# A two-block transformer forward pass on one core: the order in which the first modulation tiles, the query latents and the context's sum of squares run

## The chip, the cores and the metric

One core of a Trainium2 chip runs the whole kernel. The metric is the device time of one execution in microseconds (us). Engines: TensorE (PE in the profile, its weight loads PEld), VectorE (DVE), ScalarE (ACT), GpSimd (POOL), and the queue SP, which only issues transfers here.

## What is computed

The reference runs two transformer blocks over 256 tokens of width 1024, all in float32. The first block, cut to what matters here:

```
sh1, sc1, g1, sh2, sc2, g2 = split(silu(c) @ w_mod + b_mod)          # w_mod is 1024 x 6144
csh1, csc1, ...            = split(silu(c_ctx) @ w_mod + b_mod)
hx = rmsnorm(x,   g_attn) * (1 + sc1)  + sh1                         # 256 x 1024
hc = rmsnorm(ctx, g_attn) * (1 + csc1) + csh1                        # 256 x 1024
q_lat, na_q                      = split(hx @ w_in[:, :896])         # 384 + 512, queries: x alone
kv_lat, k_rope, na_k, na_v       = (hx and hc) @ w_in[:, 896:]       # 256 + 32 + 512 + 512
q = rmsnorm(q_lat) @ w_uq;  k, v = rmsnorm(kv_lat) @ w_ukv
attention (latent and neighbourhood), output projection, 16-expert MoE
```

The second block (spatial gating, forgetting attention, a convolutional feed-forward) follows. The change touches only the start: everything up to `kv_lat`.

## The kernel before

Activations lie feature-major: `xT` and `ctxT` are 8 tiles (`KD = 8`, index k) of 128 features by 256 tokens. Weights stream from HBM through a ring of six slots of 2 MiB (`ring`, `slot_of`); the queue SP issues the loads in a written order, and before a slot is used again it waits until its last reader is done (`through`). Slot 2 and the upper half of slots 0 and 1 share memory with early activations.

The products with `w_in` keep float32 accuracy in three fast passes: ScalarE rounds a chunk of 1024 weights per partition to a high part (`chunk_to_hi`, L619), VectorE makes the rest (`chunk_to_lo`, low part L1690), and TensorE runs high x high, low x high, high x low (`tile_product`, L1037). The activation is split in the same way: VectorE scales (`normed`, L1727), ScalarE adds the shift and rounds (`shifted`, L631), VectorE makes the low part (`shifted_lo`, L1734). A query tile has 256 columns, a tile of keys or values has 512 (x and context side by side).

At the start, in the order of the engines' programs:

- SP issues xT, the four modulation tiles `w_mod[0..3]` (shift of features 0 to 511, shift of 512 to 1023, then scale of the same two), ctxT, the part `ql` of `w_in` (384 columns, 1536 KB, into the slot of `w_mod[0]`), `kvl`, the constants, `naq`, and so on.
- TensorE multiplies a modulation tile with silu(c) and silu(c_ctx) (`mod_stream`, L978: 8 products in four column strips), each tile into a bank of its own. ScalarE copies a bank out (L612), TensorE sums the strips and puts features on partitions with a two-column matrix (`mod_pick`, L987). After the first tile it sums the squares of x with a matrix of ones (L997), after the last pick the squares of the context (L997 again), whose squares VectorE made (L1710).
- VectorE then forms `mod` (L1713) and `A1` (L1715) for all 8 tiles at once, scales x, makes the low parts of three weight chunks, makes the low parts of x, and does the same for the context.
- The list `PROD` sets the order of the products: 3 query latent tiles (`ql`), 2 key-value latent tiles (`kvl`), the rope keys (`kr`), 4 neighbourhood query tiles (`naq`), 4 of keys (`nak`), then values, and the second level. The result of product n goes to bank n % 4 and is copied out by ScalarE or VectorE ("A" or "D" in the list) before product n + 4 may write it. Chunk c + 4 is split once the product that used chunk c is done.

Of the kernel before, what the change touches and what calls it, by code (L numbers as in the profile page):

```python
# [5 lines left out]
P = 128  # L6
T = 256
# [28 lines left out]
L_QL, L_KVL, L_NAQ, L_NAK, L_NAV, L_UQ, L_UKV = range(4, 11)  # L36
# [37 lines left out]
def columns(widths):  # L74
    at, out = 0, {}
    for name, w in widths:
# [9 lines left out]
CON, NCON = columns([("upper", 128), ("ones", 128), ("pick", 2), ("pick8", 8), ("pick20", 20), ("ident", 128), ("tri", 128),  # L86
# [6 lines left out]
PROD = ([("ql", i, "AD"[i % 2]) for i in range(3)] + [("kvl", 0, "D"), ("kvl", 1, "A"), ("kr", 0, "D")]  # L93
        + [("naq", i, "AD"[i % 2]) for i in range(4)]
# [5 lines left out]
N_BEFORE_LAT = 10  # L100
W_IN = {"ql": (0, QL), "kvl": (QL, 288), "naq": (QL + 288, 512), "nak": (QL + 800, 512), "nav": (QL + 1312, 512)}
# [83 lines left out]
def block_pair_kernel(nc, xT_d, ctxT_d, vec_d, row_d, con_d, w_mod, w_in, w_uq, w_ukv, bias_d, w_out,  # L185
                      wr_d, w_gate, w_up, w_down, w_in2, wf_d, sgw_d, w_out2, w_up2, w_down2, gfin_d, out_d):
    with ExitStack() as ctx:
# [123 lines left out]
        pick = con[:, CON["pick"]:CON["pick"] + 2]  # L311
# [52 lines left out]
        squares, squared = [sem("squares0")], sem("squared")  # L364
# [46 lines left out]
        def through(n):  # L411
# [4 lines left out]
            if n < 4:  # L416
                return mod_streamed, n + 1
# [14 lines left out]
            return wide_lo, 4 * (n - L_UP + 1)  # L432

# [23 lines left out]

        NAV_DONE = [p[:2] for p in PROD].index(("nav", 3)) + 1
        UQ_FIRST = [p[:2] for p in PROD].index(("ur", 0))


        @block.sync
        def _(sp):
            def issue(n, src, cols=SLOT):
# [3 lines left out]
                sp.dma_start(ring[:, slot_of(n), 0:cols], src).then_inc(  # L468
# [13 lines left out]
            issue(L_NAQ, *w_in_part("naq"))  # L482
# [58 lines left out]
        def _(pool):  # L541

# [46 lines left out]
        def _(act):  # L589
# [17 lines left out]
            nc.scalar.activation(hT[:, :, 0:T], xT[:, :, :], ACT.Square).then_inc(squares[0], 1)  # L607
            act.wait_ge(var, NORM_STEP[0] + 1)
            nc.scalar.activation(rstd[:, 0:T], rstd[:, 0:T], ACT.Sqrt).then_inc(std, 1)
            for half in range(4):  # L610
                act.wait_ge(mod_streamed, half + 1)
                nc.scalar.activation(modp[:, half * 512:(half + 1) * 512], bank[half][:, :], ACT.Copy  # L612
                                     ).then_inc(mod_copied, 1)
# [8 lines left out]
            for c in range(3):  # L622
                chunk_to_hi(0, CHUNK1, c)
# [340 lines left out]
        def _(pe):  # L964
            def slot(n, k):

                return ring[:, slot_of(n), 0:SLOT // k * k].rearrange("p (k n) -> p k n", k=k)
# [1364 lines left out]
```

## Time and profile before

| what | value |
|---|---|
| median of 3 runs | 834.27 us (831.6 to 839.86) |
| the profiled execution's own time | 834.69 us |
| its span in the profile | 832.9 us |
| mean granted TensorE clock over the span | 0.972 of full speed |
| PE busy | 783.2 us (94%) |
| DVE / ACT / POOL busy | 394.8 / 309.4 / 21.7 us |
| moved by DMA | 198.89 MB, mean 239 GB/s |

Some 1.8 us of the execution's time lie outside the span. Rows of a timeline give start, duration, engine, line, operation, output <- inputs and count; in brackets, how long the engine had been idle and what released it. A matmul in float32 appears as two instructions. "DMA share" is the busy share of the 16 DMA engines; "PEclk" is the clock that TensorE was granted, 1.00 being 2.4 GHz and 0.50 being 1.2 GHz.

### The profile page before, as it was taken

How to read it: one execution, taken by the hardware profiler on the slowest of the kernel's cores; microseconds unless marked ns; L12 is line 12 of the kernel's file. 1: busy time of each engine (PE TensorE's matmuls, PEld its weight loads, DVE VectorE, ACT ScalarE, POOL GpSimd, SP SyncE). 2: the span in 40 equal slices, each digit the busy share in tenths (PEclk: the TensorE clock that was granted, in tenths of full speed). 3: DMA queues.
4: the chain of work that ended last, by engine and by line, in shares of the span. 5: the costliest groups of instructions: out<-in, count | busy, mean ns of one | idle time of the engine just before them, and what ended most of it. 6: DMA issues, size and time to landing. Idle time of an engine off the chain costs nothing.

```text
span 832.9 us, 11883 instructions
## 1 busy us (share of the span) xinstructions
PE 783.2 (94%) x4693; PEld 562.7 (68%) x4694; DVE 394.8 (47%) x709; ACT 309.4 (37%) x564; POOL 21.7 (3%) x22
## 2 busy tenths in 40 slices
PE   4899999999996999999999999998799999999997
PEld 1588884444784535553554448886698999999885
DVE  0685404578544101111110126766646788888543
ACT  2453103556533101100110125655344666666443
POOL 0000010030000000000000000010000000000000
PEclk9999999999996999999999998999898999999999
DMA  9934113986266799999999994204300455475401
GB/s 377 417 124 196 55 46 119 357 318 242 102 252 260 308 384 430 430 428 429 429 429 428 427 428 188 102 1 160 144 26 13 191 203 201 172 297 237 152 0 52
DMA packets 15637, 198.89 MB, mean 239 GB/s; under 512 B 1744, under 2 KB 2128, under 8 KB 3184
## 3 DMA queue, kind: packets, MB, share of 16 engines
q1 hardware_dynamic: 14688, 194.80, 57.9%
q0 software_dynamic: 624, 3.28, 1.0%
q8 instruction: 26, 0.43, 0.2%
q10 hardware_dynamic: 288, 0.30, 0.1%
q14 instruction: 11, 0.09, 0.0%
HBM read 197.31 MB, written 1.05 MB: 238 GB/s over the span
## 4 chain that ended last, share of the span: by engine, by line
PE 81%; DMA 6%; DVE 6%; ACT 5%; issue 1%; DVEq 0%; SPq 0%; ACTq 0%
PE banks L1383 12%; PE banks L1037 8%; PE banks L1641 7%; PE banks L1409 6%; PE banks L1616 5%; PE banks L1624 5%; PE banks L1620 5%; PE banks L1354 4%; PE banks L1365 3%; DMA ring<-in_w_up 3%; PE banks L1185 3%; DVE w_lo L1690 2%; PE banks L978 2%; DMA ring<-in_w_in 2%; ACT w_hi L619 2%; PE banks L1205 2%
## 5 line engine op out<-in xcount | busy, mean ns | idle before, releaser
L1690 DVE TENSOR_TENSOR w_lo<-ring,w_hi 128x1024 fp32r<-128x1024 f32 x119 | 144.8, 1223 | 92.0 <-ACT w_hi L619 44.9
L1383 PE MATMUL banks<-ring,att 128*64 128x512 f32 x512 | 111.7, 593 | 3.3 <-DVE att L2001 2.0
L1383 PEld LDWEIGHTS banks<-ring,att 128*64 128x64 f32 x512 | 36.7, 137 | 76.4 <-issue 73.1
L619 ACT ACTIVATE w_hi<-ring 128x1024 fp32r<-128x1024 f32 x53 | 54.9, 1052 | 42.4 <-PE banks L1037 28.2
L1409 PE MATMUL banks<-ring,att 128*64 128x512 f32 x256 | 56.7, 595 | 0.6 <-DVE att L2016 0.6
L2014 DVE TENSOR_TENSOR att<-att,banks 128x512 f32<-128x512 f32 x8 | 5.5, 688 | 103.6 <-PE banks L1383 103.6
L1616 PE MATMUL banks<-h_hi,w_hi 128*128 128x256 f32 x352 | 51.7, 287 | 0.3 <-ACT h_hi L913 0.3
L890 ACT ACTIVATE w_hi<-ring 128x1024 fp32r<-128x1024 f32 x44 | 46.2, 1052 | 14.1 <-PE banks L1624 14.1
L1624 PE MATMUL banks<-h_lo,w_hi 128*128 128x256 f32 x352 | 50.2, 286 | 0.0
L1620 PE MATMUL banks<-h_hi,w_lo 128*128 128x256 f32 x352 | 49.8, 284 | 0.0
L1616 PEld LDWEIGHTS banks<-h_hi,w_hi 128*128 128x128 f32 x352 | 46.3, 194 | 2.0 <-ACT h_hi L913 1.2
L1624 PEld LDWEIGHTS banks<-h_lo,w_hi 128*128 128x128 f32 x352 | 46.2, 195 | 0.0
L1620 PEld LDWEIGHTS banks<-h_hi,w_lo 128*128 128x128 f32 x352 | 45.7, 193 | 0.0
L1409 PEld LDWEIGHTS banks<-ring,att 128*64 128x64 f32 x256 | 17.7, 137 | 33.6 <-issue 32.8
L978 PE MATMUL banks<-ring,cs 128*32 128x512 f32 x192 | 26.0, 665 | 13.8 <-DMA ring<-in_w_mod 13.8
L1365 PE MATMUL banks<-arena,osb 128*128 (+1 forms) x256 | 32.1, 287 | 4.1 <-DVE arena L1986 4.1
L791 ACT ACTIVATE arena<-banks 128x256 f32 (+1 forms) x8 | 3.1, 384 | 86.8 <-PE banks L1395 86.8
L1354 PEld LDWEIGHTS banks<-arena 128*128 128x128 f32 x144 | 26.6, 190 | 11.6 <-issue 8.3
L1354 PE MATMUL banks<-arena 128*128 (+1 forms) x144 | 33.5, 385 | 1.0 <-DVE arena L2021 1.0
L1365 PEld LDWEIGHTS banks<-arena,osb 128*128 128x128 f32 x256 | 31.3, 203 | 4.3 <-DVE arena L1986 4.3
L789 ACT ACTIVATE att<-banks 128x512 f32<-128x512 f32 x8 | 4.8, 597 | 76.9 <-PE banks L1383 76.9
L895 ACT ACTIVATE w_hi<-ring 128x1024 fp32r<-128x1024 f32 x22 | 23.2, 1059 | 26.9 <-PE banks L1641 25.9
(339 smaller groups left out, 1377.9 us busy)
## 6 DMA issues: line engine op xcount, KB each, us to landing
ring<-in_w_up SPq DMA_DIRECT2D x27, 2048.0 KB, 13.4
ring<-in_w_down SPq DMA_DIRECT2D x21, 2048.0 KB, 12.3
ring<-in_w_gate SPq DMA_DIRECT2D x16, 2048.0 KB, 13.3
ring<-in_w_mod SPq DMA_DIRECT2D x12, 2048.0 KB, 9.7
ring<-in_w_in SPq DMA_DIRECT2D x8, 2048.0 KB, 13.6
ring<-in_w_out SPq DMA_DIRECT2D x4, 2048.0 KB, 7.9
arena<-in_bias POOLq DMA_DIRECT2D x2, 1024.0 KB, 9.9
ring<-in_w_in SPq DMA_DIRECT2D x1, 1536.0 KB, 18.2
```

What stands on the lines that cost most here:

```text
L619: nc.scalar.activation(chunk_part(w_hi, chunk, c), chunk_src(chunk, c), ACT.Copy).then_inc(chunk_hi[stage], 1)
L890: nc.scalar.activation(granule(w_hi, j, half), up_half_of(j, half), ACT.Copy).then_inc(wide_hi, 1)
L1037: last = nc.tensor.matmul(dst, chunk_part(part, chunk, c)[:, k, :], x[:, k, :], start=(part is w_hi and x is x_hi and k == 0), stop=(x is ...
L1354: last = nc.tensor.matmul(yacc(m), ysb[:, m * P:(m + 1) * P], place[:, i, :], start=False, stop=False, skip_group_check=True)
L1365: last = nc.tensor.matmul(bank[k // 4][:, (k % 4) * P:(k % 4 + 1) * P], h2tok[:, q, k * P:(k + 1) * P], arena[:, bass.ds(at + q * 1024, P) ...
L1383: last = nc.tensor.matmul(bank[2 + j][CAP * e:CAP * (e + 1), :], xs[:, k, CAP * e:CAP * (e + 1)], slot(n + e, KD)[:, k, :], start=(k == 0) ...
L1409: last = nc.tensor.matmul(bank[2 + half][CAP * e:CAP * (e + 1), :], hidT[:, f, CAP * e:CAP * (e + 1)], slot(L_MOE + 4 + e, 4)[:, f, half * ...
L1616: nc.tensor.matmul(dst, granule(w_hi, j, g)[:, k, :], h2_hi[:, k, :], start=(k == 0), stop=False)
L1620: nc.tensor.matmul(dst, granule(w_lo, j, g)[:, k, :], h2_hi[:, k, :], start=False, stop=False)
L1624: last = nc.tensor.matmul(dst, granule(w_hi, j, g)[:, k, :], h2_lo[:, k, :], start=False, stop=(k == KD - 1))
L1641: return nc.tensor.matmul(ytok(q, half)[:, :], x[:, kt, q * P:(q + 1) * P], part[:, kt // 2 % 2, kt % 2, half * 512:(half + 1) * 512], sta ...
L1690: return V.tensor_tensor(dst, src, high.bitcast(F32), ALU.subtract)
```

## The change

- The modulation tiles are loaded and multiplied in the order 0, 2, 1, 3 (`MOD_ORDER`): shift and scale of the first 512 features, then shift and scale of the last 512. The two tiles of a half go to the same bank, the second two rows lower (`row` = 2), so that one copy and one pick with a four-column matrix (`pick4`) serve both. The third tile loaded goes to the upper half of `arena` (`home`).
- `ql` is loaded ahead of the modulation tiles, and `naq` ahead of `kvl`. In `PROD`, `naq` stands ahead of `kvl` and `kr`. The slots up to the experts move on by one accordingly.
- The squares of x are summed ahead of all modulation tiles. VectorE makes the low parts of the three `ql` chunks ahead of the modulation, then forms `mod` and `A1`, scales and splits x by halves (k = 0 to 3, then 4 to 7). TensorE runs the first half of the first query latent tile between tile 2 and tile 3 of the modulation, the first halves of the other two between tile 3 and tile 4, and the second halves behind the last pick.
- The context's squares are made on ScalarE (between the second copy of the modulation and the shifts of k = 4 to 7), summed over k on GpSimd in three steps (4, 2 and 1 tiles of 256 columns), and only the last tile goes through TensorE, behind the third query latent product (n = 3). The context is scaled and split by VectorE and ScalarE while the `naq` products run.
- The sums of the latents' squares come ahead of product 12, not 10.

The diff, cut to its core:

```diff
-L_QL, L_KVL, L_NAQ, L_NAK, L_NAV, L_UQ, L_UKV = range(4, 11)
+L_QL, L_MOD, L_NAQ, L_KVL, L_NAK, L_NAV, L_UQ, L_UKV = 0, 1, 5, 6, 7, 8, 9, 10
+MOD_ORDER = (0, 2, 1, 3)
-        return (3, 4, 5, 2,  3, 4, 5, 3, 4, 5, 3,  4, 5, 3, 4, 5, 3, 4, 5,  3, 4)[n]
+        return (3,  4, 5, 2, 4,  5, 3, 4, 5, 3, 4,  5, 3, 4, 5, 3, 4, 5, 3,  4, 5)[n]
-PROD = ([("ql", i, "AD"[i % 2]) for i in range(3)] + [("kvl", 0, "D"), ("kvl", 1, "A"), ("kr", 0, "D")]
-        + [("naq", i, "AD"[i % 2]) for i in range(4)]
+PROD = ([("ql", i, "AD"[i % 2]) for i in range(3)] + [("naq", i, "AD"[i % 2]) for i in range(4)]
+        + [("kvl", 0, "D"), ("kvl", 1, "A"), ("kr", 0, "D")]
-N_BEFORE_LAT = 10
+N_BEFORE_LAT = 12
+        def home(n):
+            return arena[:, 4096:8192] if n == L_MOD + 2 else ring[:, slot_of(n), :]
             sp.dma_start(xT[:, :, :], xT_d).then_inc(in_x, 16)
+            issue(L_QL, *w_in_part("ql"))
             for n in range(4):
-                issue(n, w_mod[n])
+                issue(L_MOD + n, w_mod[MOD_ORDER[n]])
             sp.dma_start(ctxT, ctxT_d).then_inc(in_ctx, 16)
-            issue(L_QL, *w_in_part("ql"))
+            issue(L_NAQ, *w_in_part("naq"))
             issue(L_KVL, *w_in_part("kvl"))
...
+            for n in (4, 2, 1):
+                pool.wait_ge(ctx_sq, {4: 1, 2: 2, 1: 3}[n])
+                nc.gpsimd.tensor_tensor(hT[:, 0:n, T:2 * T], hT[:, 0:n, T:2 * T], hT[:, n:2 * n, T:2 * T], ALU.add
+                                        ).then_inc(ctx_sq, 1)
...
+            def mod_copy(half):
+                act.wait_ge(mod_streamed, 2 * half + 2)
+                nc.scalar.activation(modp[:, half * 512:(half + 1) * 512], bank[4 + half], ACT.Copy).then_inc(mod_copied, 1)
+            for c in range(3):
+                chunk_to_hi(0, CHUNK1, c)
+            mod_copy(0)
+            shift(0, range(4))
+            mod_copy(1)
+            act.wait_ge(in_ctx, 16)
+            nc.scalar.activation(hT[:, :, T:2 * T], ctxT, ACT.Square).then_inc(ctx_sq, 1)
+            shift(0, range(4, KD))
+            chunk_to_hi(0, CHUNK1, 3)
...
             for n, (kind, i, e) in enumerate(PROD):
-                if n == 5:
+                if n == 2:
+                    act.wait_ge(var, NORM_STEP[0] + 2)
+                    nc.scalar.activation(rstd[:, T:2 * T], rstd[:, T:2 * T], ACT.Sqrt).then_inc(std, 1)
+                if n == 3:
+                    shift(1, range(KD))
+                if n == KVL_FIRST + 2:
...
+            pe.wait_ge(silu_c, 1)
+            pe.wait_ge(in_con, 16)
+            pe.wait_ge(x_sq, 1)
+            for k in range(KD):
+                last = nc.tensor.matmul(bank[7][:, 0:T], ones, hT[:, k, 0:T], start=(k == 0), stop=(k == KD - 1))
+            last.then_inc(sumsq, 1)
+            mod_stream(L_MOD, 4, 0, True, False)
+            mod_stream(L_MOD + 1, 4, 2, False, True)
+            mod_pick(0)
+            latent_q(0, range(4))
+            mod_stream(L_MOD + 2, 5, 0, True, False)
+            latent_q(1, range(4))
+            latent_q(2, range(4))
+            mod_stream(L_MOD + 3, 5, 2, False, True)
+            mod_pick(1)
             for n, (kind, i, _e) in enumerate(PROD):
+                if n == 3:
+                    pe.wait_ge(ctx_sq, 4)
+                    nc.tensor.matmul(bank[7][:, T:2 * T], ones, hT[:, 0, T:2 * T], start=True, stop=True).then_inc(sumsq, 1)
...
-            dve.wait_ge(in_ctx, 16)
-            V.tensor_tensor(hT[:, :, T:2 * T], ctxT, ctxT, ALU.mult).then_inc(squares[0], 1)
...
+            for c in range(3):
+                chunk_to_lo(0, CHUNK1, c)
...
+            for half in range(2):
+                modulation(half)
+                scaled_by_norm(0, range(4 * half, 4 * half + 4))
+                shifted_low(0, range(4 * half, 4 * half + 4))
+            chunk_to_lo(0, CHUNK1, 3)
...
             for n, (kind, i, e) in enumerate(PROD):
+                if n == 2:
+                    dve.wait_ge(sumsq, SUMMED[0] + 2)
+                    V.tensor_scalar(rstd[:, T:2 * T], bank[7][:, T:2 * T], 1.0 / D, EPS, ALU.mult, ALU.add
+                                    ).then_inc(var, 1)
+                if n == 3:
+                    dve.wait_ge(std, NORM_STEP[0] + 2)
+                    link(V.reciprocal(rstd[:, T:2 * T], rstd[:, T:2 * T]))
+                    scaled_by_norm(1, range(KD))
+                if n == 4:
+                    shifted_low(1, range(KD))
```

## Rows read from the trace of the kernel before

**Rows 1.** Windows of the first 60 us and of one MoE stretch: length, busy (instructions), PEclk, DMA share, GB/s

```profile
5.00:10.00 5.00, 0.00 (x0) 0.00 (x0) 0.24 (x2) 3.24 (x3) 0.00 (x0) 1.00 1.02 429
20.00:25.00 5.00, 4.77 (x44) 2.39 (x36) 1.75 (x1) 1.69 (x4) 0.00 (x0) 1.00 1.02 436
35.00:40.00 5.00, 4.52 (x15) 2.55 (x14) 5.00 (x8) 5.00 (x11) 0.00 (x0) 0.94 1.06 440
50.00:60.00 10.00, 10.00 (x68) 7.59 (x70) 6.64 (x9) 4.06 (x6) 0.00 (x0) 1.00 0.01 2
296.00:325.00 29.00, 29.00 (x154) 14.25 (x152) 3.88 (x9) 3.08 (x7) 0.00 (x0) 1.00 0.96 399
```

**Rows 2.** Timeline, 38 to 54 us: query latent tiles, context, the first key-value tile

```profile
38.32 3.25 DVE L1734 SCALAR_TENSOR_TENSOR hT_lo<-arena,mod,hT_hi 128x256 fp32r<-128x256 f32 x8
...
42.09 1.12 PE L1037 MATMUL banks<-hT_hi,w_hi 128*128 128x256 f32 x8
42.95 1.75 DVE L1724 RECIPROCAL rstd<-rstd 128x256 f32<-128x256 f32 x1
...
44.97 1.12 PE L1037 MATMUL banks<-hT_hi,w_hi 128*128 128x256 f32 x8
...
47.84 2.00 PE L1037 MATMUL banks<-hT_hi,w_hi 128*128 128x512 f32 x8
...
53.31 1.98 PE L1037 MATMUL banks<-hT_hi,w_hi 128*128 128x512 f32 x8
```

**Rows 3.** Timeline, 0 to 34 us: what the transfers release

```profile
1.21 0.45 ACTq L599 DMA_DIRECT2D con<-in_con  x1
...
6.86 1.89 ACT L607 ACTIVATE arena<-xT 128x2048 f32<-128x2048 f32 x1
11.97 3.47 PE L978 MATMUL banks<-ring,cs 128*32 128x512 f32 x16 [11.97 <-DMA ring<-in_w_mod]
...
26.56 1.92 PE L978 MATMUL banks<-ring,cs 128*32 128x512 f32 x16 [1.79 <-DMA ring<-in_w_mod]
...
29.10 2.29 DVE L1710 TENSOR_TENSOR arena<-osb 128x2048 f32<-128x2048 f32 x1 [7.30 <-DMA osb<-in_ctxT]
...
33.75 2.95 ACT L619 ACTIVATE w_hi<-ring 128x1024 fp32r<-128x1024 f32 x3 [4.60 <-DMA ring<-in_w_in]
```

**Rows 4.** Timeline, 15 to 38 us: sums of squares, modulation, scaling and splitting of x

```profile
15.37 3.72 PE L997 MATMUL banks<-arena,con 128*128 128x256 f32 x16
...
28.41 1.95 PE L987 MATMUL banks<-con,mixT 128*128 128x2 f32 x16
28.55 0.60 ACT L612 ACTIVATE mixT<-banks 128x512 f32<-128x512 f32 x1 [4.10 <-PE banks L978]
...
31.31 0.18 DVE L1713 TENSOR_TENSOR mod<-banks,vec 128x32 f32<-128x32 f32 x1
31.45 5.41 PE L997 MATMUL banks<-arena,con 128*128 128x256 f32 x16 [1.08 <-DVE arena L1710]
...
31.74 3.26 DVE L1727 SCALAR_TENSOR_TENSOR arena<-xT,A,rstd 128x256 f32<-128x256 f32 x8
...
36.61 3.29 ACT L631 ACTIVATE hT_hi<-arena,mod 128x256 fp32r<-128x256 f32 x8
```

**Rows 5.** DMA issues of the first 1.5 us: output <- input, queue, count, KB, us to landing

```profile
con<-in_con ACTq DMA_DIRECT2D x1, 143.0 KB, 10.8
```

**Rows 6.** GpSimd additions of 2048 and 1024 elements per partition, by source line (ns)

```profile
L565 POOL TENSOR_TENSOR arena<-arena,con x2: 3801/3930/4058, 167.3 to 184.4; 128x2048 f32<-128x2048 f32 x2
```
```profile
L578 POOL TENSOR_TENSOR arena<-arena,con x1: 1997/1997/1997, 549.0 to 549.0; 128x1024 f32<-128x1024 f32 x1
```

**Rows 7.** Timeline: VectorE without and beside a GpSimd addition

```profile
166.81 0.88 DVE L1829 TENSOR_SCALAR att<-att,rinv 128x512 f32<-128x512 f32 x2
...
184.40 3.80 POOL L565 TENSOR_TENSOR arena<-arena,con 128x2048 f32<-128x2048 f32 x1 [8.55 <-DMA arena<-in_bias]
...
184.57 4.31 DVE L1829 TENSOR_SCALAR att<-att,rinv 128x512 f32<-128x512 f32 x2
```

**Rows 8.** Timeline: VectorE beside a GpSimd addition, one input in PSUM

```profile
549.46 1.29 DVE L1690 TENSOR_TENSOR hid_hi<-banks,hid_lo 128x512 fp32r<-128x512 f32 x2 [1.65 <-ACT hid_lo L871]
```

**Rows 9.** Windows around a fall of the granted clock

```profile
25.70:29.10 3.40, 2.54 (x22) 1.10 (x23) 0.00 (x0) 0.55 (x1) 0.00 (x0) 1.00 1.03 430
29.10:31.40 2.30, 1.26 (x12) 1.17 (x11) 2.30 (x2) 0.05 (x1) 0.00 (x0) 1.00 1.00 419
31.40:35.60 4.20, 4.15 (x12) 3.36 (x13) 4.13 (x11) 1.85 (x2) 0.00 (x0) 0.60 1.00 408
```

**Rows 10.** Timeline: VectorE's first and last instructions of the latents' norm

```profile
75.66 0.42 DVE L1791 TENSOR_SCALAR mixT<-banks 128x256 f32<-128x256 f32 x1 [0.37 <-PE banks L1022]
...
84.06 1.40 DVE L1801 SCALAR_TENSOR_TENSOR lat<-lat,vec,mixT 128x512 f32<-128x512 f32 x2
```

More of the change, by code:

```diff
@@ L606, in _ @@
             act.wait_ge(in_x, 16)
-            nc.scalar.activation(hT[:, :, 0:T], xT[:, :, :], ACT.Square).then_inc(squares[0], 1)
+            nc.scalar.activation(hT[:, :, 0:T], xT[:, :, :], ACT.Square).then_inc(x_sq, 1)
             act.wait_ge(var, NORM_STEP[0] + 1)
             nc.scalar.activation(rstd[:, 0:T], rstd[:, 0:T], ACT.Sqrt).then_inc(std, 1)
[L610 to L613, printed above, removed]
             def chunk_to_hi(stage, chunk, c):
@@ L985, in mod_pick @@
                 for t in range(4):
-                    c = 8 * half + 2 * t
-                    last = nc.tensor.matmul(bank[6][:, c:c + 2], modp[:, (4 * half + t) * P:(4 * half + t + 1) * P], pick,
+                    at = 16 * half + 4 * t
+                    last = nc.tensor.matmul(bank[6][:, at:at + 4], modp[:, (4 * half + t) * P:(4 * half + t + 1) * P], pick4,
                                             start=True, stop=True)
                 last.then_inc(mod_picked, 1)
-            pe.wait_ge(silu_c, 1)
-            def square_sum(part):
-                pe.wait_ge(squares[0], part + 1)
-                at = slice(part * T, (part + 1) * T)
-                for k in range(KD):
-                    last = nc.tensor.matmul(bank[7][:, at], ones, hT[:, k, at], start=(k == 0), stop=(k == KD - 1))
-                last.then_inc(sumsq, 1)
-            for half in range(4):
-                mod_stream(half, half)
-                if half == 0:
-                    pe.wait_ge(in_con, 16)
-                    square_sum(0)
-                else:
-                    mod_pick(half - 1)
-            mod_pick(3)
-            square_sum(1)
             def bank_free(prod, n, sa, sd):
@@ L1026, in _, with tile_product @@
             loads = {"ur": L_UQ, "kn": L_UKV, "vm": L_UKV}
-            def tile_product(stage, chunk, c, dst, x_hi, x_lo, hi_done, lo_done, passes=range(3)):
+            def tile_product(stage, chunk, c, dst, x_hi, x_lo, hi_done, lo_done, passes=range(3),
+                             ks=range(KD)):
                 pe.wait_ge(chunk_hi[stage], c + 1)
@@ L1033, in tile_product @@
                         pe.wait_ge(chunk_lo[stage], c + 1)
-                    for k in range(KD):
+                    for k in ks:
                         if done is not None:
@@ L1717, in _ @@
-            for s in range(2):
-                if s == 1:
-                    dve.wait_ge(sumsq, SUMMED[0] + 2)
-                    V.tensor_scalar(rstd[:, T:2 * T], bank[7][:, T:2 * T], 1.0 / D, EPS, ALU.mult, ALU.add
-                                    ).then_inc(var, 1)
-                    chunk_to_lo(0, CHUNK1, 3)
-                    dve.wait_ge(std, NORM_STEP[0] + 2)
-                    link(V.reciprocal(rstd[:, T:2 * T], rstd[:, T:2 * T]))
-                for k in range(KD):
-                    src = (xT, ctxT)[s][:, k, :]
-                    V.scalar_tensor_tensor(hT[:, k, s * T:(s + 1) * T], src, A1[:, k, s:s + 1],
+            for c in range(3):
+                chunk_to_lo(0, CHUNK1, c)
@@ new lines, in modulation, with block @@
+            def modulation(half):
+                def block(t):
+                    return t.rearrange("p (i u) c -> p i u c", i=2)[:, :, 4 * half:4 * half + 4, :]
+                dve.wait_ge(mod_picked, half + 1)
+                link(V.tensor_tensor(block(mod[:, 0:16, :]),
+                                     bank[6][:, 16 * half:16 * half + 16].rearrange("p (t i c) -> p i t c", t=4, i=2),
+                                     block(bc(v_("b_mod", 0, 16), 2, [P, 16, 2])), ALU.add))
+                ks = slice(4 * half, 4 * half + 4)
+                link(V.scalar_tensor_tensor(A1[:, ks, :], mod[:, 8 + 4 * half:12 + 4 * half, :], 1.0,
+                                            bc(v_("g_attn", 4 * half, 4), 2, [P, 4, 2]), ALU.add, ALU.mult))
```

78 lines of the change are left out of this document (35 added, 43 removed).

## The prediction

> **What bounds the kernel now.** I read the page first (PE busy 94% of the span), then windows of the start, then the timeline of that stretch, and last the windows of the MoE. For its first 40 us the core takes all that the DMA engines give, 429 to 440 GB/s at a share of 1.0, and TensorE works in pieces between arrivals; from about 40 us TensorE is busy all the time, and DMA idles [rows 1]. The reader should see the handover: until then a transfer sets the pace, afterwards every product that starts earlier ends earlier. In the MoE stretch TensorE is again full; in the code its loads wait for `used`, which TensorE raises when it is through with a slot, so a shift at the start moves them too and is carried to the end [rows 1]. So the place to measure is the moment at which the query latent tiles are done and nothing but full TensorE work follows: 47.84 us, when the first key-value tile starts [rows 2].
>
> What leads there is a chain of transfers. The first modulation tile releases TensorE at 11.97, the fourth at 26.56, the context at 29.10, `ql` only at 33.75 [rows 3]. One 2048 KB tile therefore takes (26.56 - 11.97) / 3 = 4.86 us. Then come three weight chunks on ScalarE (2.95 us) and eight shifts behind them, the first at 36.61 [rows 3, 4]; x's scaling was done at 35.0. The sum of the context's squares (31.45 to 36.86, [rows 4]) is just not late.
>
> **The change, part by part.**
>
> Transfers. `ql` in front costs the modulation 1536/2048 x 4.86 = 3.65 us: first tile at 11.97 + 3.65 = 15.6, then 20.5, 25.3 and 30.2. The matrix of ones is needed first now; it was issued at 1.21 and took 10.8 us [rows 5], so it is there at about 12. The squares of x are ready by 8.75 [rows 3], their sum takes 3.72 us at full clock and, estimated by the first stream's slowness (3.47 against 1.92 us, [rows 3]), some 1.6 more: done at 17.3, still 3 us ahead of the second tile. The fourth tile's slot is free when the first is streamed (17.3 + 1.9 = 19.2), while two tiles are queued until 25.3, so SP's wait leaves no gap. The context lands at about 32.7, `naq` at 37.6, `kvl` at 40.3, each ahead of its use below. The load into `arena` touches nothing in use. Cost of all this: nothing, hidden by the queue; if the fourth tile came over 3 us late, that would be added.
>
> First half. Tile 2 is streamed at 20.5 + 1.9 = 22.4. Before, from the end of the last stream (28.48) to the last pick's end (30.36) went 1.9 us; from the start of `mod` (31.31) to that of scaling (31.74) 0.43 [rows 3, 4]. Four scalings take 4 x 0.41 = 1.6, four low parts as much (8 in 3.26 and 3.25, [rows 2, 4]), and TensorE ends 0.3 behind: 1.9 + 0.1 + 0.4 + 1.6 + 1.6 + 0.3 = 6.0 us, so 28.4. ScalarE's three chunks (17.9 to 20.9) and VectorE's reciprocal and three low parts (to about 23.5) hide under the tile's arrival.
>
> Middle. Stream 1.9, two half tiles, stream 1.9. A query tile takes 44.97 - 42.09 = 2.88 us [rows 2], so two halves take 2.9. Together 6.7, so the fourth stream ends at t0 = 35.1, 5 us behind the tile's arrival: TensorE, not DMA, sets this.
>
> Second half. The same 6.0 us and two halves, 2.9: 44.0. Against 47.84 that is 3.8 us gained. The single context product (one of eight: 3.72/8 = 0.46 us, [rows 4]) is added: 3.4 left. Half the picks and the sum of 5.41 us vanish, but they stood under the transfer, so they count nothing more.
>
> Context squares. On ScalarE the square takes 1.89 us (as x's, [rows 3]) from the second copy's end: t0 + 0.7 to t0 + 2.6. The shift of k = 4, queued behind it, is not ready before t0 + 2.9, so this wait is covered by 0.3 us. GpSimd then adds 1024, 512 and 256 elements. 1024 take 2.00 us, 2048 take 3.80 to 4.06 [rows 6]; by the same slope the others take 1.05 and 0.55, together 3.6, ending at t0 + 6.3, while TensorE asks at t0 + 8.9. For TensorE they are hidden by 2.6 us. For VectorE they are not. Beside GpSimd's addition of 184.40 to 188.20, two tensor_scalars that take 0.88 alone took 4.31: VectorE stood until the addition was over [rows 7]. The adds start at t0 + 2.65, in the middle of VectorE's four scalings (from t0 + 2.4), on which the shifts, the low parts and TensorE wait. No row shows a scalar_tensor_tensor beside an addition. The lower bound is nothing, by the product pair that read PSUM and took 1.29 us beside an addition, 0.64 for 512 elements where 256 take 0.41 elsewhere [rows 2, 8]; the upper is all three adds, 3.6. I take 3.6: scalings read two SBUF operands and no PSUM, which is nearer to [rows 7] than to [rows 8], and each add is asked for while a scaling runs and follows it.
>
> The Trainium skill (SBUF — State Buffer, "Who interferes with whom") says that a VectorE instruction with two SBUF inputs contends with a GpSimd instruction that reads SBUF, and that the second to issue blocks until the first is done. The trace agrees for the tensor_scalar (4.31 us); that the two-input form does the same no row shows. By the rule the sum is the one here; without it, that of the first rival.
>
> Clock. In 29.10 to 31.40 TensorE did 1.26 us, all of it two-column picks, and over 31.40 to 35.60 the granted clock was 0.60 in the mean, so at 1.2 GHz for most of it [rows 9]; the sum of squares took 5.41 for 3.72, 1.7 us more [rows 4]. The stretch with a whole stream in it (25.70 to 29.10) brought no fall [rows 9]. The changed kernel has two such holes: 22.4 to 28.4, and t0 to t0 + 9.5 with the adds. In each TensorE does a few picks and products that wait for ScalarE. Bounds are 0 and 1.7 for each. The first falls partly under work that is paced by ScalarE anyway: 0.7. The second is longer and is followed by full work: 1.7. Together 2.4.
>
> Context chain. Behind the third query tile VectorE and ScalarE must do the variance, square root, chunk, reciprocal (1.75), eight scalings (3.26), a shift, chunk and copy. That is some 11.3 us, under four `naq` tiles of 4 x 2.88 = 11.5 [rows 2, 4]. Their cover is 0.2 us thick; bounds 0 and 1.5, I take 0.2, since bank 0 too comes free at about the moment when the second key-value tile asks for it. Behind it the latents' sums come two products later. VectorE's norm of the latents (75.66 to 85.46, 9.8 us, [rows 10]) stood under two tiles of keys and stands under the other two now, each 53.31 - 47.84 = 5.47 us [rows 2]: 10.9 us and then the rope products, with the first two value chunks split already. Cost nothing; its cover is 1 us and more.
>
> Sum: -3.8 + 0.4 + 3.6 + 2.4 + 0.2 = +2.8 us. Against the profiled execution (834.69) that is 837.5; it lay 0.4 above the median of the runs, so against the median 837.0.
>
> **The rivals.**
>
> 1. VectorE is not held. For it: [rows 8]. Against it: [rows 7]. Without 3.6, and with a shorter second hole (clock 0.7 + 0.6): -3.8 + 0.4 + 1.3 + 0.2 = -1.9, so 832.4. If the clock also stays up, 831.1.
> 2. GpSimd waits for VectorE instead: VectorE's instructions follow each other at once, and the adds start when its low parts are done, t0 + 5.8. They end at t0 + 9.4, TensorE's context product waits 0.5 us, the clock costs 1.9: -3.8 + 0.4 + 0.5 + 1.9 + 0.3 = -0.7, so 833.6. For it: no row shows an addition asked for amid VectorE's back-to-back work and winning.
> 3. Slower: the context chain becomes the bound. Its place is the first key-value tile (n = 7), which needs the context's shifts, chunk 7 and bank 3. It decides as soon as the chain is longer than the 11.5 us of `naq`; every us beyond is added. With the chain stretched by waits of both engines for each other's chunks (one more chunk on each, 1.0 + 1.2, and 1 us for the second tile's bank) it gives 3.2 more: 840.2. Against it: ScalarE is idle for half of such stretches [rows 1].
> 4. The change doesn't do what it says: the latents' first halves start so late that the fourth tile is streamed no earlier than `ql` was used before. The fourth tile's 5 us of slack speak against it; it would give 838 to 842.
>
> **How the numbers follow.** Forecast 0.50, rival 1 0.25, rival 2 0.12, rival 3 0.10, rival 4 0.03. The range runs from rival 1 with the clock kept (831.1) less half a us for the spread of runs, to rival 3 plus as much: 830.5 to 841.0. A measurement of this kernel can tell about 1% (8.3 us) from no change; no case passes that but for its tail, so faster 0.03, within 0.93, slower 0.04.
>
> **What would show it.** In the changed profile: the first modulation stream near 16 to 17, the fourth ending near 35; a scaling that starts near 37.8 and whose group of four takes over 5 us instead of 1.6, beside three GpSimd additions; granted clock under 1.00 in 26 to 30 and again in 38 to 44; the third query latent product ending near 50, where without holding it would be near 45; the first key-value tile starting 12 us behind it, with no PE idle ahead of it. The distance from the end of `ql` to the attention should be unchanged but for 0.46. The prediction is wrong if VectorE runs through, if the clock stays at 1.00, or if a stage behind 143 us moves by itself.

## The result, and the profile after

| | before | changed |
|---|---|---|
| median of 15 runs each, us | 834.52 (831.6 to 839.86) | 842.3 (835.44 to 844.13) |
| profiled execution, us | 834.69 | 841.15 |
| its span, us | 832.9 | 839.4 |
| mean granted clock | 0.972 | 0.964 |

The ratio is 1.0074, 95% interval 1.0051 to 1.0097: slower by 6.2 us (4.3 to 8.1), where +2.8 was forecast. It is within 1%, and the sign was right; the size was less than half of what came. The prediction's range, up to 841.0, holds the ratio applied to its own starting median (1.0074 x 834.27 = 840.4) and just misses the later median of 842.3.

The page of the changed kernel: span, busy time of TensorE and of GpSimd, and the granted clock in 40 slices of 21 us. TensorE did the same work; GpSimd has 6.5 us more than the 21.7 of before, though the three new additions are only 4.5 of that.

```profile
span 839.4 us, 11817 instructions
...
PE 784.0 (93%) x4664; PEld 563.0 (67%) x4664; DVE 398.8 (48%) x710; ACT 310.1 (37%) x563; POOL 28.2 (3%) x25
...
PEclk9889999999996999999999998999888999999999
```

The timeline of the start (start, duration, engine, line). The modulation stream is L996 now, the sum of squares L1083 and, for the context alone, L1098; picks L1005, scaling L1753, low parts L1759, weight products L1038, ScalarE's square L644, GpSimd's additions L550.

```profile
10.59 5.28 PE L1083 MATMUL banks<-arena,con 128*128 128x256 f32 x16 [10.59 <-DMA con<-in_con]
15.80 1.92 PE L996 MATMUL banks<-ring,cs 128*32 128x512 f32 x16
20.15 3.21 PE L996 MATMUL banks<-ring,cs 128*32 128x512 f32 x16 [2.42 <-DMA ring<-in_w_mod]
24.06 1.05 PE L1005 MATMUL banks<-con,mixT 128*128 128x4 f32 x8 [0.70 <-ACT mixT L630]
25.57 1.67 DVE L1753 SCALAR_TENSOR_TENSOR arena<-xT,A,rstd 128x256 f32<-128x256 f32 x4
30.06 2.31 PE L996 MATMUL banks<-arena,cs 128*32 128x512 f32 x16
35.37 1.92 PE L996 MATMUL banks<-ring,cs 128*32 128x512 f32 x16
37.85 1.90 ACT L644 ACTIVATE arena<-osb 128x2048 f32<-128x2048 f32 x1
39.51 5.24 DVE L1753 SCALAR_TENSOR_TENSOR arena<-xT,A,rstd 128x256 f32<-128x256 f32 x4
39.84 4.63 POOL L550 TENSOR_TENSOR arena<-arena 128x1024 f32<-128x1024 f32 x3 [39.37 <-ACT arena L644]
44.68 1.66 DVE L1759 SCALAR_TENSOR_TENSOR hT_lo<-arena,mod,hT_hi 128x256 fp32r<-128x256 f32 x4
50.54 0.60 PE L1098 MATMUL banks<-arena,con 128*128 128x256 f32 x2
62.48 2.00 PE L1038 MATMUL banks<-hT_hi,w_hi 128*128 128x512 f32 x8
147.26 1.95 PE L1211 MATMUL banks<-arena,big 128*128 128x512 f32 x4 [0.83 <-issue]
```

Against [rows 2 to 4]: the four scalings of the first half take 1.67 us, the same four of the second half 5.24, over nearly the same stretch as GpSimd's additions. The query latents end at about 50.4 where they ended at 47.84, and attention (L1211) starts at 147.26 where L1185, the same line in the kernel before, started at 144.09: +3.2.

```profile
144.09 2.38 PE L1185 MATMUL banks<-arena,big 128*128 128x512 f32 x5 [0.83 <-issue]
```

The rest of the 6.2 us comes later.

The windows around the two stretches in which TensorE has little to do, for comparison with [rows 9]: us, then busy time of PE, PEld, DVE, ACT and POOL (instructions), granted clock, DMA share, GB/s.

```profile
17.80:20.15 2.35, 0.00 (x0) 0.00 (x0) 2.31 (x3) 1.83 (x2) 0.00 (x0) 1.00 1.05 446
20.15:23.40 3.25, 3.21 (x16) 0.54 (x16) 1.96 (x2) 0.00 (x0) 0.00 (x0) 0.58 0.98 418
...
26.70:30.00 3.30, 3.25 (x12) 2.65 (x12) 2.12 (x6) 1.09 (x3) 0.00 (x0) 0.62 0.96 407
40.60:45.30 4.70, 1.52 (x3) 0.76 (x3) 4.70 (x5) 1.53 (x4) 3.71 (x3) 0.56 1.04 370
45.30:47.40 2.10, 2.05 (x9) 2.06 (x10) 2.10 (x4) 0.94 (x1) 0.00 (x0) 0.50 0.93 398
```

The clock falls twice in the first 30 us: under the second stream, behind 2.35 us in which TensorE did nothing (granted clock 1.00 there, 0.58 in the stream), and again about 26.7. The groups of GpSimd's additions, kept apart by shape (busy us, mean ns of one):

```profile
L575 POOL TENSOR_TENSOR arena<-arena,con 128x2048 f32<-128x2048 f32 x2 | 9.1, 4530 | 19.1 <-DMA arena<-in_bias 19.1
L588 POOL TENSOR_TENSOR arena<-arena,con 128x1024 f32<-128x1024 f32 x1 | 2.4, 2414 | 304.0 <-ACT arena L845 304.0
...
L550 POOL TENSOR_TENSOR arena<-arena 128x1024 f32<-128x1024 f32 x1 | 2.4, 2360 | 39.4 <-ACT arena L644 39.4
L550 POOL TENSOR_TENSOR arena<-arena 128x512 f32<-128x512 f32 x1 | 1.3, 1331 | 0.1
L550 POOL TENSOR_TENSOR arena<-arena 128x256 f32<-128x256 f32 x1 | 0.8, 787 | 0.1
```

L575 and L588 are L565 and L578 of [rows 6], untouched by the change: they took 3930 and 1997 ns and take 4530 and 2414.

### The profile page after: what moved, and what is told of

Read it like the earlier page. It is cut to its first block, busy times and chain, and to the rows that moved or that the text cites. A ratio compares the mean times of both kernels' runs of the same rounds, so it can differ in the third digit from the quotient of the medians.

```text
span 839.4 us, 11817 instructions
## 1 busy us (share of the span) xinstructions
PE 784.0 (93%) x4664; PEld 563.0 (67%) x4664; DVE 398.8 (48%) x710; ACT 310.1 (37%) x563; POOL 28.2 (3%) x25
## 4 chain that ended last, share of the span: by engine, by line
PE 77%; DMA 10%; DVE 6%; ACT 5%; issue 1%; SPq 0%; DVEq 0%; ACTq 0%
PE banks L1409 11%; PE banks L1038 8%; DMA ring<-in_w_up 8%; PE banks L1667 7%; PE banks L1642 5%; PE banks L1646 5%; PE banks L1650 5%; PE banks L1435 4%; PE banks L996 3%; PE banks L1380 3%; PE banks L1211 3%; PE banks L1391 2%; DVE w_lo L1716 2%; DMA ring<-in_w_mod 2%; ACT w_hi L625 2%; PE banks L1220 2%
## 5 line engine op out<-in xcount | busy, mean ns | idle before, releaser
L1409 PE MATMUL banks<-ring,att 128*64 128x512 f32 x512 | 113.6, 600 | 3.1 <-DVE att L2042 2.0
L1435 PE MATMUL banks<-ring,att 128*64 128x512 f32 x256 | 56.7, 595 | 0.6 <-DVE att L2057 0.6
L1038 PE MATMUL banks<-hT_hi,w_hi 128*128 128x256 f32 (+1 forms) x104 | 23.8, 360 | 6.4 <-ACT hT_hi L635 6.4
```

The lines of the kernel that those rows point to most:

```text
L1038: last = nc.tensor.matmul(dst, chunk_part(part, chunk, c)[:, k, :], x[:, k, :], start=(part is w_hi and x is x_hi and k == 0), stop=(x is ...
L1409: last = nc.tensor.matmul(bank[2 + j][CAP * e:CAP * (e + 1), :], xs[:, k, CAP * e:CAP * (e + 1)], slot(n + e, KD)[:, k, :], start=(k == 0) ...
L1435: last = nc.tensor.matmul(bank[2 + half][CAP * e:CAP * (e + 1), :], hidT[:, f, CAP * e:CAP * (e + 1)], slot(L_MOE + 4 + e, 4)[:, f, half * ...
```

## The experiments

Differences in us are (ratio - 1) x 835; each kernel is compared with runs of the kernel before on its own chip.

### Do the additions hold VectorE?

**No additions.** The changed kernel with GpSimd's three additions left out; TensorE's single context product then takes the first 128 features' squares alone.

```
-            for n in (4, 2, 1): ... gpsimd.tensor_tensor(...)
-                    pe.wait_ge(ctx_sq, 4)
+                    pe.wait_ge(ctx_sq, 1)
```

> The three GpSimd additions of the context's squares are left out (the sum takes the squares of the first 128 features only, so the context's norm is another one); all else is as in the changed kernel. Theory (the additions hold VectorE's four scalings): the group of four scalings falls from 5.24 us to 1.67, the third query latent product ends about 3.6 us earlier or a little more by the clock (near 46.5 instead of 50.4), and the kernel takes about 4 to 5 us less than the changed one, 0 to +0.3% of the kernel before. Rival (the scalings are slow by their own place in the order, or the loss is made by the clock alone): the group stays over 4 us and the time within 1 us of the changed kernel, +0.7%.

Measured: 836.34 us, ratio 1.0012 [0.9982, 1.0041]. Timeline of the second half:

```profile
38.61 1.67 DVE L1749 SCALAR_TENSOR_TENSOR arena<-xT,A,rstd 128x256 f32<-128x256 f32 x4
...
46.16 0.60 PE L1094 MATMUL banks<-arena,con 128*128 128x256 f32 x2
```

The group takes 1.67 us again, 3.57 less than 5.24. From the fourth stream's end to the end of the query latents it is 46.04 - 36.38 = 9.66 us, where the changed kernel took 50.42 - 37.29 = 13.13: 3.47 less. So the holding is the whole of what this stretch loses to the additions: the longer hole that it makes costs at most 0.1 us of clock beyond.

**The square earlier.** In ScalarE's program the context's square goes ahead of the second copy of the modulation, so that the additions fall into the stretch before the scalings. Nothing is left out.

```
             mod_copy(0)
             shift(0, range(4))
-            mod_copy(1)
             act.wait_ge(in_ctx, 16)
             nc.scalar.activation(hT[:, :, T:2 * T], ctxT, ACT.Square).then_inc(ctx_sq, 1)
+            mod_copy(1)
             shift(0, range(4, KD))
```

> ScalarE squares the context ahead of the second copy of the modulation, when the context has landed (32.4), not behind it; the additions then start near 34.4 and end near 38.1. Theory: only the last 0 to 0.8 us of them meet the scalings (from 39.5 in the changed kernel, when the copy isn't delayed), the group takes 1.7 to 2.4 us, the third query latent product ends near 46.5 to 47, and the time is 3.5 to 5 us under the changed kernel's, -0.1 to +0.4% of the kernel before. Rival (what holds VectorE is any GpSimd work near it, or the additions cost elsewhere when moved, on the copy or on the weight chunks): the gain is under 1.5 us, at least +0.6% of the kernel before.

Measured: 835.4 us, ratio 1.0001 [0.9978, 1.0024]. Timeline:

```profile
32.48 1.91 ACT L643 ACTIVATE arena<-osb 128x2048 f32<-128x2048 f32 x1 [5.89 <-DMA osb<-in_ctxT]
...
34.48 4.50 POOL L550 TENSOR_TENSOR arena<-arena 128x1024 f32<-128x1024 f32 x3 [34.01 <-ACT arena L643]
...
38.27 2.17 DVE L1753 SCALAR_TENSOR_TENSOR arena<-xT,A,rstd 128x256 f32<-128x256 f32 x4
```

The same additions, the same work: only the 0.7 us at which the last addition overlaps the first scaling are held (2.17 for 1.67). The query latents end at 45.96, 1.9 us ahead of the kernel before.

**More additions.** Two more of 1024 elements ahead of the three, written to a free tile; the result is not changed. Shortened:

```
+            pool.wait_ge(ctx_sq, 1)
+            for n in range(2):
+                nc.gpsimd.tensor_tensor(att[...], hT[:, 0:4, T:2 * T], hT[:, 4:8, T:2 * T], ALU.add) ...
             for n in (4, 2, 1):
```

> Two more GpSimd additions of 1024 elements per partition (2.0 us each) into unused memory, ahead of the three. Theory: VectorE is held once more for each, so the scalings and the low parts of the second half take about 4 us more together, and the third query latent product ends 4 us later, near 54.4, the kernel at 4 to 5 us more than the changed one, +1.2 to +1.4% of the kernel before. Rival (GpSimd only got in once, before VectorE's queue was full): VectorE's groups stay as they are, and at most the context's product waits, for 1 us or less.

Measured: 844.2 us, ratio 1.0115 [1.0078, 1.0151]. Timeline:

```profile
38.53 7.93 DVE L1758 SCALAR_TENSOR_TENSOR arena<-xT,A,rstd 128x256 f32<-128x256 f32 x4
38.86 4.84 POOL L550 TENSOR_TENSOR att<-arena 128x1024 f32<-128x1024 f32 x2 [38.40 <-ACT arena L649]
...
43.78 4.69 POOL L555 TENSOR_TENSOR arena<-arena 128x1024 f32<-128x1024 f32 x3
```

VectorE gets one instruction in per addition: four scalings and the start of the low parts are stretched over five additions, 7.93 us for 1.67, and the low parts 3.15 for 1.66. The first key-value tile comes at 65.2, 2.7 later than in the changed kernel, in which the stage had started about 1 us later.

**TensorE sums the context.** The additions are left out and TensorE does all 8 products of the sum behind the third query latent.

```
-                    nc.tensor.matmul(bank[7][:, T:2 * T], ones, hT[:, 0, T:2 * T], start=True, stop=True)
+                    for k in range(KD):
+                        nc.tensor.matmul(bank[7][:, T:2 * T], ones, hT[:, k, T:2 * T], start=(k == 0), stop=(k == KD - 1))
```

> No GpSimd additions; TensorE sums all eight tiles of the context's squares behind the third query latent product, 3.7 us instead of 0.46. Theory: the 3.6 us of holding go, 3.3 us of TensorE come, the first key-value tile starts at about the same time or up to 1 us earlier for the shorter hole (61.5 to 62.4), and the time is within 1.5 us of the changed kernel's, +0.5 to +0.8% of the kernel before. Rival (holding isn't the loss): 3.3 us more than the changed kernel, +1.1%.

Measured: 840.85 us, ratio 1.0064 [1.0035, 1.0092]. Scalings take 1.67 us; the first `naq` product starts at 48.95, 1.8 before the changed kernel's. The eight products take 3.4 us (from the first weight load at 45.56 to the next product's at 48.92) where the single one took 0.3 (50.42 to 50.76), on an engine that is full from there on. The first key-value tile came at 60.65, ahead of the 61.5 to 62.4 that was expected. So moving the sum to GpSimd is worth having, if its additions lie where VectorE isn't wanted.

### What do the holes cost in clock?

**TensorE kept busy.** The early square and a shift of the constants (below), and 12 products of the matrix of ones with x into a bank that is free: four behind the first stream, one ahead of and three behind each of the two picks.

> As the kernel with both edits, with twelve further products of ones and x into an unused bank: four between the first two modulation tiles, one ahead of each pick, three behind each pick, 0.46 us each, in stretches where TensorE had waited. Theory (the clock falls because TensorE does little in these holes): the granted clock stays 1.00 from 16 us on, the third modulation stream takes 1.92 instead of 2.28 us and more, the first halves less, and the first key-value tile starts 1 to 2 us earlier than at 58.0; the time is 1 to 2 us less than without. Rival (the holes don't matter for the clock, or the products stand in the way): the tile starts at the same time or up to 1 us later.

Measured: 835.22 us, ratio 0.9983 [0.9957, 1.0009]. Timeline:

```profile
17.78 1.99 PE L1076 MATMUL banks<-xT,con 128*128 128x256 f32 x8
...
20.43 1.92 PE L996 MATMUL banks<-ring,cs 128*32 128x512 f32 x16 [0.65 <-DMA ring<-in_w_mod]
...
33.11 1.92 PE L996 MATMUL banks<-ring,cs 128*32 128x512 f32 x16
```

With the hole filled the second stream takes 1.92 us, not 3.21, and the fourth ends at 35.03, where the sum at full clock said 35.1 and the changed kernel needed until 37.29. That is what the clock took in the first 37 us of the changed kernel's profiled execution: 2.2 us.

Other executions lose less there, without any filling. The early-square kernel (timeline):

```profile
10.64 6.33 PE L1083 MATMUL banks<-arena,con 128*128 128x256 f32 x16 [10.64 <-DMA con<-in_con]
...
20.22 1.92 PE L996 MATMUL banks<-ring,cs 128*32 128x512 f32 x16 [1.40 <-DMA ring<-in_w_mod]
```

In six traces without filling (no additions, early square, more additions, TensorE sums, padded, early and padded) the first sum took 6.1 to 6.7 us, TensorE then stood 1.0 to 1.7 us ahead of the second stream, and that stream took 1.92 or 1.93. Their fourth stream ended at 36.0 to 36.4: the clock took 1.0 to 1.3 us. In two (the changed kernel and the early, padded kernel with pieces) the sum took 5.3 and 5.1 us, TensorE stood 2.4 and 2.6 us, the second stream took 3.21 and 3.56, and the fourth ended at 37.3 and 37.4. The filled kernel began like these two (sum 5.15 us), so it is with them that it is compared.

The filling did not keep the clock in the second half. From the fourth stream's end to the end of the query latents it took 11.3 us (35.03 to 46.33), where the early-square kernel took 9.9 (36.05 to 45.96): the granted clock was 0.50 from 42 to 44, and the scalings, which start earlier, now meet 2 us of the additions (3.05 us for 1.67). So the first key-value tile comes at 58.38, not 1 to 2 us ahead of 58.0 as was expected, and in total the filling brings nothing that can be told from the same kernel without it (0.997 [0.9947, 0.9993], below).

### Where do the other 3 us come from?

In the table of constants the pick matrix grew from 2 columns to 4, and everything behind it moved by 8 bytes, among it the mask and the triangle that GpSimd adds in both attentions.

**The kernel before with a wider pick.** Only this:

```
-CON, NCON = columns([("upper", 128), ("ones", 128), ("pick", 2), ...
+CON, NCON = columns([("upper", 128), ("ones", 128), ("pick", 4), ...
```

> The kernel before with one edit: the pick matrix has four columns (two of them unused), so that all constants behind it, the mask and the triangle among them, and all tensors behind the constants lie 8 bytes further on, as in the changed kernel. Theory (in the changed kernel GpSimd's additions are slower because of where their operands now lie): the additions of 1024 elements take 2.41 us instead of 2.00 and the two of the bias 4.5 instead of 3.8, VectorE is held 0.5 to 0.7 longer by each bias addition, and the kernel takes 1 to 3 us more than before, +0.1 to +0.35%. Rival (GpSimd is slower for another reason, the new program of the queue or what ran before): they stay at 2.00 and 3.8 to 4.06, and the time is that of before.

Measured: 838.85 us, ratio 1.0029 [1.0007, 1.0052]: 2.4 us slower, with no instruction changed. Its groups:

```profile
L565 POOL TENSOR_TENSOR arena<-arena,con 128x2048 f32<-128x2048 f32 x2 | 9.0, 4518 | 18.2 <-DMA arena<-in_bias 18.2
L578 POOL TENSOR_TENSOR arena<-arena,con 128x1024 f32<-128x1024 f32 x1 | 2.4, 2409 | 301.5 <-ACT arena L827 301.5
```

**The changed kernel with two unused columns** behind the new pick matrix (`("pick4", 4), ("pad", 2), ...`).

> The changed kernel with two unused columns behind the four-column matrix, so that the constants lie at 8 bytes off a multiple of 64, as before. Theory: the additions with the mask and the triangle take 2.00 and 3.8 to 4.06 us again, the three of the context (both operands in arena) stay at 2.36 for 1024 elements; the time falls by 1 to 3 us against the changed kernel, to +0.4 to +0.65% of the kernel before; the start of the first key-value tile stays at 62.4. Rival: nothing changes, +0.74%.

Measured: 837.44 us, ratio 1.0006 [0.998, 1.0032]. Its groups:

```profile
L575 POOL TENSOR_TENSOR arena<-arena,con 128x2048 f32<-128x2048 f32 x2 | 7.6, 3803 | 18.3 <-DMA arena<-in_bias 18.3
L550 POOL TENSOR_TENSOR arena<-arena 128x1024 f32<-128x1024 f32 x1 | 2.4, 2360 | 38.4 <-ACT arena L644 38.4
...
L588 POOL TENSOR_TENSOR arena<-arena,con 128x1024 f32<-128x1024 f32 x1 | 2.0, 1998 | 302.2 <-ACT arena L845 302.2
```

The additions with a constant are fast again, and the one of 1024 elements with both inputs in `arena` keeps its 2360 ns. The time came lower than the +0.4 to +0.65% that was expected. The triangle starts at column 414 before, 416 in the two slow tables and 418 here. Whether the distance between the two inputs decides or the place of each, these runs don't separate. The additions inside `arena`, whose inputs lie 8192, 4096 and 2048 bytes apart, don't settle it: they read no constant repeated over the tile, and they were run in one placement only.

**Early square and padding together.**

> Both: the square ahead of the second copy and the two unused columns. Theory: the first key-value tile starts at 58.0, the additions later are short, and the time is 1 to 3 us under that of the square made early alone (+0.01%), -0.35 to -0.1% of the kernel before. Rival (what is lost behind the start comes from the new order or from chance): it stays within 1 us of the kernel before.

Measured: 833.82 us, ratio 0.997 [0.9947, 0.9993]: 2.5 us faster than the kernel before.

### Why do a few hundred ns of addition matter so much?

In the first attention each of the two mask additions meets the scaling of the attention weights, as [rows 7] showed for one. In the profile of the early, padded kernel TensorE stands for it (timeline):

```profile
185.94 3.80 POOL L575 TENSOR_TENSOR arena<-arena,con 128x2048 f32<-128x2048 f32 x1 [8.71 <-DMA arena<-in_bias]
185.97 4.47 DVE L1870 TENSOR_SCALAR att<-att,rinv 128x512 f32<-128x512 f32 x2
...
190.09 1.97 PE L1220 MATMUL banks<-con,att 128*128 128x128 f32 x8 [2.28 <-DVE att L1870]
```

So each of the two additions was cut into four of 512 elements, in that kernel and in the kernel before:

```
-                nc.gpsimd.tensor_tensor(b, b, mask over 32 rows, ALU.add).then_inc(bias_ready, 1)
+                for part in range(4):
+                    bp = b[:, 8 * part:8 * part + 8, :]
+                    ins = nc.gpsimd.tensor_tensor(bp, bp, mask over 8 rows, ALU.add)
+                ins.then_inc(bias_ready, 1)
```

> The padded kernel with the early square, and beyond it each of GpSimd's two bias additions of 2048 elements in the first attention is cut into four of 512. If an addition holds VectorE's scaling of the attention weights for its own length, and TensorE stands for it (3.8 + 3.1 us behind two held scalings in the profile of the padded early kernel), a piece (about 1.0 us by 3.80/4) holds it for 1 us at most before VectorE gets its turn: the longest attention scaling falls from over 4 us to under 1.6, TensorE's stalls there fall to under 2 us together, and the median is 2 to 5 us under that of the padded early kernel (0.991 to 0.995 of the kernel before). If the pieces go to GpSimd back to back with no turn for VectorE in between, the scaling still takes over 4 us and the time stays within 1 us (0.997). If the attention's stalls were hidden by what TensorE has queued, scalings get short and the time still stays.

> The kernel before with the same cut of the two bias additions and nothing else. In the profiled execution of the kernel before, the first addition started at 167.30, just behind a scaling of 166.81, and the two together held it for some 5 us over two places (2.64 - 0.88 and 4.31 - 0.88). If the holds are what they cost, the median falls by 2 to 5 us (0.994 to 0.998) and the runs lie closer together; if VectorE gets no turn between pieces, or the stalls were hidden, it stays (1.000).

Measured: 831.88 us, ratio 0.9955 [0.9929, 0.9981] for the first, 833.19 us, 0.9976 [0.9952, 1.0001] for the kernel before with nothing but this cut. Timelines, first the early padded kernel with pieces, then the kernel before with them:

```profile
184.27 1.72 DVE L1872 TENSOR_SCALAR att<-att,rinv 128x512 f32<-128x512 f32 x2
184.39 4.65 POOL L577 TENSOR_TENSOR arena<-arena,con 128x512 f32<-128x512 f32 x4 [8.84 <-DMA arena<-in_bias]
```

```profile
184.48 4.59 POOL L567 TENSOR_TENSOR arena<-arena,con 128x512 f32<-128x512 f32 x4 [8.59 <-DMA arena<-in_bias]
184.61 2.46 DVE L1831 TENSOR_SCALAR att<-att,rinv 128x512 f32<-128x512 f32 x2
```

The four pieces take longer than the one (4.6 for 3.8), yet VectorE gets its turn between them: the pairs of scalings that meet an addition take 1.4 to 2.5 us, not 4.5. Against the padded early kernel the first is 1.3 us less by the two ratios, where 2 to 5 were expected; their intervals overlap. In the trace of the kernel before with pieces the first attention's scores last from 144.1 to 205.9 us, without pieces from 144.1 to 209.4. Of these 3.5 us the medians show 2.0 [-0.1 to 4.0], so no gain is shown for the kernel before, and one trace doesn't give the price. Which scaling an addition meets depends on when its 1 MB of bias lands (in the twelve traces GpSimd waited 9.0 to 10.5 us for the first).

### The account

If the start and the constants are all, a kernel's distance is that of its attention's start in the profile, plus 2.4 for the slow constants (from the wider pick), minus 2.0 for pieces:

| kernel | start | other terms | sum | measured |
|---|---|---|---|---|
| changed | +3.2 | +2.4 | +5.6 | +6.2 [4.3, 8.1] |
| no additions | -1.2 | +2.4 | +1.2 | +1.0 [-1.5, 3.4] |
| early square | -1.3 | +2.4 | +1.1 | +0.1 [-1.8, 2.0] |
| more additions | +5.9 | +2.4 | +8.3 | +9.6 [6.5, 12.6] |
| TensorE sums | +1.3 | +2.4 | +3.7 | +5.3 [2.9, 7.7] |
| padded | +2.2 | 0 | +2.2 | +0.5 [-1.7, 2.7] |
| early, padded | +0.4 | 0 | +0.4 | -2.5 [-4.4, -0.6] |
| the same, kept busy | -0.9 | 0 | -0.9 | -1.4 [-3.6, 0.8] |
| early, padded, pieces | -0.3 | -2.0 | -2.3 | -3.8 [-5.9, -1.6] |

Eight of nine lie in their interval; without the 2.4 the changed kernel, more additions and TensorE sums would fall outside. The ninth (early, padded) was profiled in its longest execution, 839.28 against its median of 833.82: the second half took 11.4 us (36.15 to 47.58) there, with a granted clock of 0.50 from 40 to 46. The term for the constants has an interval of its own (0.6 to 4.3), and the padding gave back more in the changed kernel (5.7 us between the two ratios) than it costs in the kernel before; the intervals allow one value, but don't show it.

The comparison goes by medians. The first attention's own length (first to last start of a score product) shows the constants' term in some traces and not in the one that matters most. The last score products before, with the wider pick, and in the changed kernel, whose first ones started at 144.1, 144.1 and 147.3:

```profile
L1185 PE MATMUL banks<-arena x32: 589/641/693, 175.5 to 209.4; 64*128 64x512 f32 x32
```
```profile
L1185 PE MATMUL banks<-arena x32: 589/641/693, 177.2 to 212.0; 64*128 64x512 f32 x32
```
```profile
L1211 PE MATMUL banks<-arena x32: 589/641/693, 178.7 to 211.8; 64*128 64x512 f32 x32
```

The attention lasts 65.3 us before and 67.9 with the wider pick. It lasts 67.6 to 67.8 in the four kernels with the slow table of the first group of experiments, and 64.3 to 66.4 in the three padded ones with whole additions. In all of these but the kernel before, both additions hold a pair of scalings for most of their length. In the changed kernel's own trace, as in that of before, the first addition came at the end of one pair and held the next for a part only (3.41 us, 2.64 before), the granted clock over 143 to 216 was 1.00 where it had been 0.96, and the attention lasted 64.5. So in this trace the distance of +3.2 has shrunk to +0.8 at the MoE's first gather (260.6 against 259.8), and 5.7 us of the two spans' 6.5 arise behind it. What makes them is open: from that gather to the second attention's first scores the twelve traces took between 294 and 298 us, in no order that follows the edits.

## Why the prediction was right and where it was not

- **The handover** was the right place to measure. The first key-value tile came 12 us behind the third query latent, at 62.48, with TensorE busy throughout, and from the end of the latents to attention it was 96.9 us where it had been 96.3: the forecast was +0.46.
- **The order of the transfers** came as said: second tile's stream at 20.15 (20.5). The first stream, forecast behind the sum of squares at 17.3, started at 15.80, because the constants were there at 10.59 and not at 12.
- **Holding VectorE**: +3.6 forecast, 5.24 - 1.67 = 3.57 in the trace and 3.47 by the kernel without additions. The size came out right because two errors cancel: the additions last 4.63 us, not 3.6 (2360, 1331 and 787 ns and the gaps), and some 1.06 us of scaling goes on beside or between them (1.67 less the 0.33 ahead of the first addition and the 0.28 behind the last). The rule of the Trainium skill (SBUF — State Buffer, "Who interferes with whom") was weighed beside it; the trace agrees with it now for the two-input form as well (5.24 us for 1.67). The kernel with more additions adds that one held instruction gets in ahead of each next addition. Rival 1 falls by this row. Rival 2 falls too: the first addition starts at 39.84, amid VectorE's back-to-back work.
- **The clock**: 2.4 forecast in two holes, 2.2 + 0.8 measured, but not where I put it. The first 37 us lost 2.2 instead of 0.7: 1.3 of it in the second stream, behind a stretch that I had overlooked (17.80 to 20.15), in which TensorE has nothing at all; in the trace of before the sum of squares stood there. It is 2.35 us long here because the sum was done early; in the six traces in which it was done near 17 us, as forecast, the first 37 us lost 1.0 to 1.3. The second cost 9.66 - 8.9 = 0.8 instead of 1.7, with or without the holding; by other executions (the early, padded kernel's 11.4 us with 0.5 of holding) it can be 2.0. In this trace the two errors cancel to 0.6, and that they do so is luck.
- **The context chain** cost 0 (0.2 forecast), so rival 3 falls, and rival 4 with it: the streams and halves ran in the order written. The measured 840.4 lies where these two had put the time (840.2, and 838 to 842), but by neither of their mechanisms.
- **The sum at the start**: +2.8 forecast, +3.2 measured at the attention's start. The mechanism was right, and the closeness of the number is in part luck: the errors in the holding and in the clock cancel.
- **What failed** is the step "The change part by part": it cost the four-column pick matrix at nothing, by not costing it at all. It asked for each tile that the change touches, and not for those that it moves. The wider matrix moved the masks of two attentions, GpSimd's additions on them became 15 to 21% longer, and by the wider pick in the kernel before that is 2.4 [0.6, 4.3] of the missing 3.4 us; the padding, the same test in the changed kernel, gave back 5.7. That the longer additions cost this by holding VectorE fits the attention's lengths above, but the changed kernel's own trace doesn't show it. The prediction's own list of what would make it wrong ended with "if a stage behind 143 us moves by itself": that is what happened. Of the remaining 1.0 us 0.4 is the start; the rest is within the interval and stays unexplained. The premise that a shift at the start is carried to the end holds for the sums of the account by medians; in the changed kernel's trace the distance went from 3.2 to 0.8 to 6.5 us.

## What to carry to other kernels

An addition on GpSimd is not free because GpSimd is idle: look at what VectorE does in that stretch, put it where VectorE waits anyway, or cut it so that VectorE gets its turn; moving one ScalarE instruction up took back the holding. A diff that changes the width of anything in a packed table moves all that lies behind it, so compare the untouched groups of the engine too, ahead of explaining the rest by the change. Where an order of work is changed, count each stretch in which TensorE is left without a product, since the clock is paid in the work behind it, and look at several executions: what such a stretch cost differed by 1 us between them.

## What the runs showed of the hardware that was not expected

- GpSimd's addition of 1024 float32 per partition takes 2.00 or 2.41 us, of 2048 3.80 to 4.07 or 4.50 to 4.72, by an 8-byte shift of one input. With both inputs in `arena` 1024 took 2.36.
- Under a run of additions VectorE's two-input instructions go at one per addition (four took 7.93 us and reached over four of the five additions, which took 4.84 + 4.69 us).
- Four additions of 512 take 4.6 us where one of 2048 takes 3.8, and yet they hold VectorE less: the attention's second addition held scalings for 1.6 to 1.7 us in pieces and for 3.4 to 3.6 whole.
- An idle stretch of 2.35 us ahead of a stream was followed by granted clock 0.58 and a stream of 3.21 us for 1.92; with products in it the stream took 1.92, and so it did without them in six traces in which TensorE stood 1.0 to 1.7 us.
